# One layer's stick-breaking attention: sums from softplus halves, one item later, and the second branch moved behind the output gate

## The reference

```
z       = where(key before query, q . k / sqrt(128), -1e30)
sums    = sum over j >= key of softplus(z[j])
weights = exp(z - sums)
out_b   = weights @ v
merged  = sigmoid(gate_a) * (a @ w_branch_a) + sigmoid(gate_b) * (out_b @ w_branch_b)
```

## Time and profile before

| | |
|---|---|
| time, median of 3 runs | 2600.06 us (2599.68 to 2600.07) |
| span of the profiled execution | 2597.7 us |
| PE busy, share of the span | 2586.5 us, 100% |
| weight loads busy | 2211.3 us, 85% |
| DVE busy | 2028.6 us, 78% |
| ACT busy | 1544.6 us, 59% |
| POOL busy | 121.4 us, 5% |
| chain that ended last, share on PE | 97% |
| mean granted TensorE clock | 1.000 |

### The profile page before, as it was taken

The page is one execution under the profiler, slowest core; times in us unless marked ns, Lnnn a source line. Parts: engine busy times, 40 slices in busy tenths (PEclk is TensorE's granted clock), DMA queues, the critical chain, the costliest instruction groups (busy, mean ns, idle before and its releaser), DMA issues.

```text
span 2597.7 us, 34900 instructions
## 1 busy us (share of the span) xinstructions
PE 2586.5 (100%) x14184; PEld 2211.3 (85%) x14184; DVE 2028.6 (78%) x2078; ACT 1544.6 (59%) x1703; POOL 121.4 (5%) x148
## 2 busy tenths in 40 slices
PE   9999999999999999999999999999999999999999
PEld 7889998888888899888888889978888889988887
DVE  8887754698799686557998995676997996677987
ACT  6556774465565567645656555555656555655654
POOL 0000170000000004400000000000000000000000
PEclk9999999999999999999999999999999999999999
DMA  8646444466465555545747465544755646544662
GB/s 260 227 152 214 155 155 170 145 227 225 150 230 173 171 164 166 178 143 178 237 164 233 161 204 181 161 146 154 243 195 188 209 162 189 161 146 148 215 229 105
DMA packets 354876, 475.03 MB, mean 183 GB/s; under 512 B 28758, under 2 KB 279966, under 8 KB 354462
## 3 DMA queue, kind: packets, MB, share of 16 engines
q1 hardware_dynamic: 349246, 469.86, 55.1%
q10 hardware_dynamic: 4416, 1.90, 0.3%
q0 software_dynamic: 1056, 1.05, 0.3%
HBM read 467.13 MB, written 5.64 MB: 182 GB/s over the span
## 4 chain that ended last, share of the span: by engine, by line
PE 97%; ACT 1%; DVE 1%; DMA 0%; SPq 0%; issue 0%; DVEq 0%; ACTq 0%
PE bank L421 29%; PE bank L423 29%; PE bank L422 29%; PE bank L1020 1%; PE bank L565 1%; PE bank L1909 1%; PE bank L1885 1%; DMA raw<-in_ffn_w_in 0%; PE bank L2790 0%; PE bank L2737 0%; PE bank L2726 0%; ACT w_hi L402 0%; PE bank L1833 0%; PE bank L1832 0%; PE bank L1856 0%; PE bank L2747 0%
## 5 line engine op out<-in xcount | busy, mean ns | idle before, releaser
L421 PE MATMUL bank<-w_hi,xn_hi 128*128 128x512 f32 (+2 forms) x1856 | 704.4, 380 | 1.4 <-DVE xn_lo L537 0.8
L423 PE MATMUL bank<-w_hi,xn_lo 128*128 128x512 f32 (+2 forms) x1856 | 691.9, 373 | 0.0
L422 PE MATMUL bank<-w_lo,xn_hi 128*128 128x512 f32 (+2 forms) x1856 | 691.0, 372 | 0.0
L408 DVE TENSOR_TENSOR w_lo<-raw,w_hi 128x2048 fp32r<-128x2048 f32 (+2 forms) x190 | 411.6, 2168 | 217.3 <-ACT w_hi L402 216.7
L1157 ACT ACTIVATE w_hi<-raw 128x2048 fp32r<-128x2048 f32 x192 | 367.3, 1913 | 135.6 <-DMA raw<-in_ffn_w_out 39.7
L402 ACT ACTIVATE w_hi<-raw 128x2048 fp32r<-128x2048 f32 (+2 forms) x198 | 358.0, 1809 | 147.8 <-PE bank L423 146.6
L1265 DVE TENSOR_TENSOR w_lo<-raw,w_hi 128x2048 fp32r<-128x2048 f32 x192 | 438.4, 2284 | 1.0 <-ACT w_hi L1157 0.9
L421 PEld LDWEIGHTS bank<-w_hi,xn_hi 128*128 128x128 f32 x1856 | 349.7, 188 | 64.5 <-issue 5.2
L423 PEld LDWEIGHTS bank<-w_hi,xn_lo 128*128 128x128 f32 x1856 | 349.5, 188 | 61.3
L422 PEld LDWEIGHTS bank<-w_lo,xn_hi 128*128 128x128 f32 x1856 | 350.0, 189 | 56.4
L421 PE MATMUL bank<-w_hi,hid_hi 128*128 128x512 f32 x704 | 278.1, 395 | 0.0
(11 more groups left out here) (404 smaller groups left out, 3922.8 us busy)
## 6 DMA issues: line engine op xcount, KB each, us to landing
raw<-in_w_in SPq DMA_DIRECT2D x122, 1024.0 KB, 5.2
raw<-in_ffn_w_in SPq DMA_DIRECT2D x126, 512.0 KB, 5.4
raw<-in_ffn_w_out SPq DMA_DIRECT2D x44, 1024.0 KB, 5.2
raw<-in_ffn_w_down SPq DMA_DIRECT2D x44, 1024.0 KB, 5.2
raw<-in_ffn_w_gate SPq DMA_DIRECT2D x64, 512.0 KB, 4.3
raw<-in_ffn_w_up SPq DMA_DIRECT2D x64, 512.0 KB, 5.3
block<-in_ffn_w_in SPq DMA_DIRECT2D x48, 512.0 KB, 7.6
block<-in_ffn_w_gate SPq DMA_DIRECT2D x24, 512.0 KB, 6.6
```

Source lines behind the costliest of these rows:

```text
L408: dve.tensor_tensor(in_order(kind, slot, w_lo), as_loaded(kind, slot), in_order(kind, slot, w_hi).bitcast(F32), ALU.subtract).then_inc(s_l ...
L421: pe.matmul(out, a_hi, b_hi, start=start, stop=False, skip_group_check=check)
L422: pe.matmul(out, a_hi, b_lo, start=False, stop=False, skip_group_check=check)
L423: return pe.matmul(out, a_lo, b_hi, start=False, stop=stop, skip_group_check=check)
```

## The change

Six things are changed.

1. The sums of a pair are made from halves. ACT copies the softplus of both heads, 128 x 768, to float32r (`soft_hi`), DVE subtracts it and gets `soft_lo`. PE then does for each head and each half one float32r pass of 384 columns with the triangle and one of 128 columns with the ones: 8 float32r passes for a pair, in place of 6 float32 products.
2. The sums of a pair stand behind item SBK+5, the product with v behind SBK+6, the weights on ACT at SBK+6 and the results on ACT and DVE at SBK+7: all one item later. The halves are made at SBK+4. There is one tile of each half, so ACT's copy waits until PE is done with the sums of the pair before (`s_R`).
3. Items 31 and 32 are now the output gate `z` and items 33 to 36 are branch b's projection.
4. The triangle and the ones are converted to float32r once, at the start of the first mixer.
5. A wait for a free PSUM bank counts the second of a pair of value items.
6. The scratch of POOL's own DMAs is reduced to 4096 bytes, which makes room for the new tiles.

```diff
-        + [("gb", (8208 + 512 * n, h)) for n in range(2) for h in range(2)] + [("b", (512 * n, h)) for n in range(2) for h in range(2)]
-        + [("z", (3584, h)) for h in range(2)] + [("ga", (7184 + 512 * n, h)) for n in range(2) for h in range(2)] + [("a", (0, 0))])
+        + [("gb", (8208 + 512 * n, h)) for n in range(2) for h in range(2)] + [("z", (3584, h)) for h in range(2)]
+        + [("b", (512 * n, h)) for n in range(2) for h in range(2)] + [("ga", (7184 + 512 * n, h)) for n in range(2) for h in range(2)] + [("a", (0, 0))])
...
             dve.tensor_copy(ident_r[:, :], ident)
+            dve.tensor_copy(tri_r[:, :], C["neg_tri"])
+            dve.tensor_copy(all_r[:, :], C["neg_ones"])
...
                 if j in BANK_USERS:
-                    wait_read(pe, l, BANK_USERS[BANK_USERS.index(j) - 2])
+                    former = BANK_USERS[BANK_USERS.index(j) - 2]
+                    wait_read(pe, l, former + (former in UNREAD1))
...
+                    if j == SBK[r] + 6:
+                        stick_out_pe(pe, l, r)
                     if j == SBK[r] + 5:
-                        stick_out_pe(pe, l, r)
-                    if j == SBK[r] + 4:
                         stick_sums_pe(pe, l, r)
...
         def stick_sums_pe(pe, l, r):
             for i in range(2):
-                b, w = stick_bank(r, i), sticks[r % 2][:, i, :]
-                pe.wait_ge(s_sp, l * 8 + (2 * r + i + 1))
-                for out, m, src in ((slice(0, 256), "neg_tri", w[:, 0:256]),
-                                    (slice(128, 256), "neg_ones", w[:, 256:384]),
-                                    (slice(256, 384), "neg_tri", w[:, 256:384])):
-                    mm = pe.matmul(b[:, out], C[m], src, start=False, stop=True, skip_group_check=True)
+                b = stick_bank(r, i)
+                if i == 0:
+                    pe.wait_ge(s_splo, l * 4 + (r + 1))
+                for half_ in (soft_hi, soft_lo):
+                    pe.matmul(b[:, 0:384], tri_r[:, :], half_[:, i, :], start=False, stop=True, skip_group_check=True)
+                    mm = pe.matmul(b[:, 128:256], all_r[:, :], half_[:, i, 256:384], start=False, stop=True,
+                                   skip_group_check=True)
                 mm.then_inc(s_R, 1)
...
                 for r in range(4):
+                    if j == SBK[r] + 7:
+                        stick_out_act(act, l, r)
                     if j == SBK[r] + 6:
-                        stick_out_act(act, l, r)
-                    if j == SBK[r] + 5:
                         stick_weights_act(act, l, r)
+                    if j == SBK[r] + 4:
+                        stick_halves_act(act, l, r)
...
+        def stick_halves_act(act, l, r):
+            act.wait_ge(s_sp, l * 8 + (2 * r + 2))
+            if l or r:
+                act.wait_ge(s_R, l * 8 + 2 * r)
+            act.activation(soft_hi[:, :, :], sticks[r % 2][:, :, :], ACT.Copy).then_inc(s_sphi, 1)
...
                 if 1 <= j <= LATE and j != GATES_ACT:
                     split_lo(dve, pm, j + 2)
+                for r in range(4):
+                    if j == SBK[r] + 4:
+                        stick_halves_dve(dve, l, r)
                 if LATE <= j < N1 - 3:
                     split_lo(dve, pm, j + 3)
...
+        def stick_halves_dve(dve, l, r):
+            dve.wait_ge(s_sphi, l * 4 + (r + 1))
+            dve.tensor_tensor(soft_lo[:, :, :], sticks[r % 2][:, :, :], soft_hi[:, :, :].bitcast(F32),
+                              ALU.subtract).then_inc(s_splo, 1)
...
-    nc = bacc.Bacc("TRN2", target_bir_lowering=False, num_devices=1)
+    nc = bacc.Bacc("TRN2", target_bir_lowering=False, num_devices=1, dynamic_dma_scratch_size=4096)
```

More of the change, by code:

```diff
@@ L258, in build @@
         shared = top[0]
+        beyond = shared + 94208
         gate_act = put("gate_act", [NT, 256], at=shared)
@@ L1506, in build @@
         sticks = [put("stick0", [2, 384], at=gain_at), put("stick1", [2, 384], at=shared + 86016)]
+        soft_hi = put("soft_hi", [2, 384], F32R, at=beyond + 6144)
+        soft_lo = put("soft_lo", [2, 384], F32R, at=beyond + 9216)
+        tri_r = put("neg_tri_r", [P], F32R, at=beyond + 5120)
+        all_r = put("neg_ones_r", [P], F32R, at=beyond + 5632)
         small_at = shared + 89088
@@ L1572, in build @@
         s_sp = sem("stick_softplus")
+        s_sphi = sem("stick_softplus_hi")
+        s_splo = sem("stick_softplus_lo")
         s_R = sem("stick_sums")
@@ L2238, in mixer1_dve @@
                 for r in range(4):
-                    if j == SBK[r] + 6:
+                    if j == SBK[r] + 7:
                         stick_out_dve(dve, l, r)
```

## The result

The changed kernel takes **2606.95 us** (median of 8 runs, 2605.32 to 2609.28), the kernel before 2599.91 us beside it (8 runs, 2599.34 to 2600.45). The ratio is 1.0028, with an interval of 1.0019 to 1.0037: slower, by 7 us. The profiled execution took 2609.28 us, the slowest of the eight, and its span is 2607.5 us against 2597.7.

What follows compares the result with a forecast made beforehand. PE's passes bound the kernel, with step 0 nearly waiting for the inverses' load. Terms 1.6 + 3.6 + 1.6 = 6.8 us on the 2597.7 us span gave 2604.5, so 2607 us; range 2604.2 to 2610.7, with rivals 2601 to 2611.

Steps and rivals of the forecast that it cites:

- What bounds the kernel: PE's passes bound it; the delta rule's step 0 nearly waits for the inverses' load, margins 0.4 and 0.2 us.
- Part 1, the sums: PE's sums: a pair takes 1.1 us instead of 1.75, saving 0.6, from passes of 0.17 and 0.11 us.
- Part 2, one item later: PE reaches step 0 3.6 us earlier but waits; pair 3's sums, now behind the landing, add 1.6 us in all.
- Part 3, the halves: DVE's new subtractions block POOL's solve, so the inverses land later: 1.8 us a layer, 3.6 us in two.
- rival A: POOL's solve isn't delayed, the inverses land as before and the clock holds: 2601.7 us, chance 0.20.
- Part 4, the clock: At PE's two waits for the inverses, one clock fall of two was taken: 1.6 us (0 to 3.2).
- B: The wait for the inverses at step 0 doesn't bind, so PE's saving counts: 2595.3 or 2593.8 us, chance 0.09.
- C: Item 29's low half collides with POOL's copy, which waits 2.2 us more per layer: about 2611 us, chance 0.09.
- Parts 5 and 6: Output gate order, step 3's wait, constants' casts, bank wait and POOL's own transfers: all put at nothing.

Runs made afterwards that it cites:

- the second profile: The changed kernel run once more, unedited: median 2607.62 us of 6 runs, the profiled execution 2607.47 us.

## Why the prediction was right, and where it was not

The forecast was 2607 us and slower, and 2606.95 was measured. The mechanism was the one foreseen; the agreement of the number is better than that of its terms. Two small things in the sums: the terms of the range add up to 2604.1 to 2610.6 us, 0.1 less than was written, and what lies around the span is about 1.8 us in the executions that followed, not 2.4. The profiled execution of before was thus most likely some 0.6 us below the median, and the forecast stands.

- **What bounds the kernel.** Right. The margins of 0.4 and 0.2 us at step 0, which no list of waits shows, decided the sign. With the load out of the way the same change is worth 4.7 us.
- **Part 1, the sums.** 1.1 us for a pair were foretold and measured, from passes of 0.17 and 0.11 us that were wrong one by one: 0.17 to 0.23 for 384 columns, 0.06 for 128. The low bound from columns alone, 0.07, was the right one for the short pass, and the weight load that had spoken against it did not show.
- **Part 2, one item later.** Right: 2 x 1.1 - 0.6 = 1.6 us, and the arrival at 386.5 us where 386.4 was said.
- **Part 3, the halves.** The blocking was right, and rival A with it wrong. Its price was 1.8 us a layer at the landing. In layer 0 the landing moved by about 1.7 us (389.65 to 391.35), though by another sum: the copy was 2.4 us late, and the load took 0.7 us less (6.2 in place of 6.9). In layer 1 it moved only 0.4 us against the layer's own start, though the copy was 1.8 us late there too, since the turned store ahead of it took 1.93 us where it had taken 3.04 before:

```profile
1072.58 3.04 SPq L1709 DMA_DIRECT2D inv_t_scratch<-diag_inverse_t  x4
```

  So this term was oversized: 2.2 us in two layers in place of 3.6, and about 1.2 in the second profile, where step 0 came 0.3 us late in each layer. The delay of GpSimd itself was close to the 1.8 us a layer of the forecast, but only in the mean. Its copy in layer 0 starts 1.2 to 2.4 us later than 378.10 in the six profiles of kernels that have both the subtraction and the new place of the sums. But 378.10 is no constant either: the two other kernels from before without the subtraction have 377.34 and 379.20. The steadier measure is the time from GpSimd's last operation ahead of the solve to the copy. In the seven profiles with the subtraction it is 71.2 to 72.3 us in layer 0 and 70.3 to 71.3 in layer 1, in the five without it 69.1 to 70.8 and 68.7 to 69.5, so 1.7 us more in the mean of either layer. In the changed kernel's layer 0 three operations are stretched by 0.53 us each, one beside each subtraction; the first is shown above, these are the other two (0.61 and 0.52 us for the same sizes before):

```profile
347.12 1.15 POOL L2557 TENSOR_TENSOR outer<-diag_blocks,diag_inverse 64x252 f32<-64x252 f32 x1
373.26 1.06 POOL L2560 TENSOR_TENSOR diag_inverse<-diag_inverse,outer 64x175 f32<-64x175 f32 x1
```

- **Part 4, the clock.** This step failed. I took one fall of two and 1.6 us for it. The clock fell at both waits, and a fall cost 1.6 to 3.1 us: 5.5 us in the first profile, 4.1 in the second, in place of 1.6. Two readings were at fault. "4.3 us after" was read from the end of the program, as if a stretch of standing still had to be that long; in layer 1 the clock fell 2.4 us after PE's last matmul, and waits of 2.4 to 2.5 us were enough at the branch's items. And the start of the program, where 1.6 us went, is not the price here: step 0 and item 29 ran at half speed for longer. The rule of the Trainium skill that I had set against my choice, that activity is what releases the clock (TensorE: Matmul & The Clock Gate, section "What's actually happening"), spoke for both waits, and the trace agrees with it.
- **Rivals.** A is excluded by the copy and by the experiment without the subtraction, though its number, 2601.7, is nearly that experiment's median, 2601.6. That agreement is partly luck: the one profile of it without a fall took 2598.95 us. B's case was made by hand: the load that comes early gives 2595.1 us, and 2595.3 was its number. C did not come: GpSimd's copy took 2.10 us, as before.
- **Parts 5 and 6.** The order was put at nothing. That holds for the new order: it is worth nothing in the kernel before, and the old one would have cost 12.5 us in the changed one. The prediction had given the need for it as its reason.

The terms, then: 1.6 + 2.2 + 5.5 us in the first profile and 1.6 + 1.2 + 4.1 in the second, where 1.6 + 3.6 + 1.6 stood. The landing was put too high and the clock too low. The first profile is the slowest of its eight executions, 2.3 us above the median, so the terms of an ordinary one are nearer to the second. That the total met the median is partly luck.

## What to carry to other kernels

Where an engine is busy all the time, look for what it nearly waits for: set each start against the landing of its operands, and ask whether what you save lies ahead of that point or behind it. A wait on TensorE costs its length and, behind every profiled one of 2.4 us or more in the middle of these kernels, 1.3 to 3.1 us more of passes at half speed. If a short wait can't be removed, take its cause forward in the queue: here one transfer, moved ahead of four stores in its queue and away from a load of weights, turned a loss of 7 us into a gain of 4.7.

## What the runs showed of the hardware that was not expected

- **The place in a queue changes a transfer's time.** The same load of 512 KB takes 6.1 to 7.0 us behind the turned stores and the next weights (1 MB, issued about 0.55 us ahead of it), and 3.4 to 3.6 us ahead of the stores, with those weights issued earlier; its issue takes 0.34 us instead of 0.51 to 0.53. Whether the stores or the weights beside it make the difference was not tested apart.
- **The clock and short waits.** These are the waits of TensorE at step 0 and at the branch's items: in those of 1.2, 1.7, 1.8 and 2.2 us of the profiled executions the clock stayed at 1.00; with those of 2.4 to 2.5, 3.2, 3.7, 4.0, 4.8 and 4.9 us it fell to 0.50, in the wait or shortly behind it. With the wait of 4.9 us it fell about 5.3 us after the last matmul had ended, in the one of 3.65 us after 2.4 us, and with one of 2.5 us when the passes had run again for 1.6 us. Where it falls is not a fixed time behind the last matmul. Nor do the profiles show that a wait of 2.2 us is safe: the mean clocks of the other executions of that kernel speak against it.
- **Two subtractions in a row hold GpSimd twice.** VectorE's subtraction of 768 columns takes 0.95 us at best and up to 1.44 us beside GpSimd. The operation of GpSimd beside it takes 0.99 us in place of 0.46, directly behind one that was held for 2.29 us. The Trainium skill (SBUF — State Buffer, section "Who interferes with whom") has the one that comes second blocked to the other's end; the trace agrees in the main. VectorE's subtraction ran from 329.71 to 330.88, GpSimd's operation came at 330.21 and ended at 331.20, 0.32 us behind it, which is a little less than its own 0.46. So the price was 0.5 us, and not the subtraction's full length.
- **More work, less time.** 18 passes a layer that nobody reads took 3.1 us off the median.
